# State-space units issued to TensorE in pairs, with the B and C transposes and chunk 8 moved

## The reference, cut to what matters

```
h = x * (1 + sc_m) + sh_m
u, q, k, v, g_out, a_low = jnp.split(h @ w_in[layer], IN_SPLITS, axis=-1)
y_s5  = _s5_group(u, ...)       # 32 groups of 16 channels, 64 complex states each
y_gla = _gla_group(q, k, v, g_out, a_low, ...)
y = jnp.concatenate([y_s5, y_gla], axis=-1) @ w_out[layer]

# in _s5_group
bu = jnp.einsum('gph,blgh->blgp', b_bar, u_c)        # B: channels to states
states = linear recurrence of bu over the sequence
y = jnp.einsum('ghp,blgp->blgh', c_mat, states).real # C: states to channels
y = jax.nn.gelu(y + d_skip * u);  return y * sigmoid(y @ w_glu + b_glu)
```

## Time and profile before

| what | value |
| --- | --- |
| median of 3 runs | 2751.89 us (2750.16 to 2752.95) |
| the profiled execution's own time | 2751.11 us |
| its span | 2749.3 us, 36615 instructions |
| PE busy | 2582.1 us, 94% of the span |
| DVE, ACT, POOL busy | 63%, 46%, 25% |
| mixer of layer 2, from the first projection matmul to the start of `y_sum(1)` | 888.12 to 997.15 us of the span |
| the same for layer 3 | 1349.90 to 1453.77 us |

### The profile page before, as it was taken

The page is one execution under the profiler, slowest core; times in us unless marked ns, Lnnn a source line. Parts: engine busy times, 40 slices in busy tenths (PEclk is TensorE's granted clock), DMA queues, the critical chain, the costliest instruction groups (busy, mean ns, idle before and its releaser), DMA issues.

```text
span 2749.3 us, 36615 instructions
## 1 busy us (share of the span) xinstructions
PE 2582.1 (94%) x14374; PEld 2086.1 (76%) x14374; DVE 1739.3 (63%) x1998; ACT 1257.4 (46%) x1300; POOL 675.9 (25%) x353
## 2 busy tenths in 40 slices
PE   7998999998999987999896699999999999999996
PEld 4775998874998754999774488888888878787884
DVE  1254665454866565665465577777777777777785
ACT  1123443223443112333112277677677777676763
POOL 0000000001920433920171122232223323222223
PEclk9998999998999998999997799999999999999997
DMA  9885764466774563875431299999999999999992
GB/s 339 274 282 192 253 215 143 153 217 204 242 228 153 174 209 123 265 226 184 124 113 35 70 364 341 357 329 367 329 369 329 359 337 348 350 348 340 344 360 106
DMA packets 434952, 693.80 MB, mean 252 GB/s; under 512 B 37690, under 2 KB 255894, under 8 KB 434838
## 3 DMA queue, kind: packets, MB, share of 16 engines
q1 hardware_dynamic: 407632, 677.17, 71.6%
q10 hardware_dynamic: 27206, 15.03, 2.0%
HBM read 691.10 MB, written 1.05 MB: 252 GB/s over the span
## 4 chain that ended last, share of the span: by engine, by line
PE 50%; issue 30%; POOL 11%; DVE 5%; ACT 2%; DMA 1%; SPq 0%; POOLq 0%; ACTq 0%; DVEq 0%
POOL ring_part L1260 10%; PE bank L656 9%; PE bank L788 9%; PE bank L790 8%; PE bank L789 8%; PE bank L560 3%; PE bank L772 3%; PE bank L670 3%; PE bank L898 1%; PE bank L543 1%; PE bank L719 1%; ACT hT L1368 1%; PE bank L918 1%; PE bank L751 1%; PE bank L633 1%
## 5 line engine op out<-in xcount | busy, mean ns | idle before, releaser
L1368 ACT ACTIVATE region_part<-ring 128x2048 fp32r<-128x2048 f32 x432 | 805.1, 1907 | 302.6 <-PE bank L790 197.7
L790 PE MATMUL bank<-ring_part,region_part 128*128 128x512 f32 x1648 | 649.1, 394 | 0.0
L2204 DVE TENSOR_TENSOR ring_part<-ring,region_part 128x2048 fp32r<-128x2048 f32 x270 | 640.4, 2404 | 2.8 <-ACT region_part L1368 2.8
L788 PE MATMUL bank<-region_part 128*128 128x512 f32 x1432 | 582.8, 407 | 6.2 <-DVE ring_part L2204 6.2
L789 PE MATMUL bank<-region_part 128*128 128x512 f32 x1296 | 512.1, 395 | 0.0
L1260 POOL TENSOR_TENSOR ring_part<-ring,region_part 128x2048 fp32r<-128x2048 f32 x54 | 268.7, 4983 | 554.5 <-ACT region_part L1368 554.5
L790 PEld LDWEIGHTS bank<-ring_part,region_part 128*128 128x128 f32 x1648 | 309.9, 188 | 71.4
L788 PE MATMUL bank<-xn_part,region_part 128*128 128x256 f32 x1152 | 327.8, 285 | 10.0 <-DVE hT_part L1924 9.1
L788 PEld LDWEIGHTS bank<-region_part 128*128 128x128 f32 x1432 | 269.7, 188 | 75.6 <-issue 14.6
L790 PE MATMUL bank<-hT_part,region_part 128*128 128x256 f32 x1152 | 326.0, 283 | 0.0
L789 PE MATMUL bank<-xn_part,ring_part 128*128 128x256 f32 x1152 | 325.7, 283 | 0.0
(11 more groups left out here) (295 smaller groups left out, 3432.1 us busy)
## 6 DMA issues: line engine op xcount, KB each, us to landing
ring<-in_moe_w_gate SPq DMA_DIRECT2D x126, 1024.0 KB, 5.1
ring<-in_moe_w_up SPq DMA_DIRECT2D x126, 1024.0 KB, 5.1
ring<-in_moe_w_down SPq DMA_DIRECT2D x126, 1024.0 KB, 5.0
ring<-in_w_ada SPq DMA_DIRECT2D x48, 1024.0 KB, 7.5
ring<-in_mod_w SPq DMA_DIRECT2D x48, 1024.0 KB, 5.3
ring<-in_w_in SPq DMA_DIRECT2D x44, 1024.0 KB, 5.7
ring<-in_w_up_act SPq DMA_DIRECT2D x22, 1024.0 KB, 5.4
ring<-in_w_up_lin SPq DMA_DIRECT2D x22, 1024.0 KB, 6.1
```

The costliest lines, as they stand in the source:

```text
L788: nc.tensor.matmul(o, split(a_hi), split(b_hi), start=start, stop=False, skip_group_check=True)
L790: return nc.tensor.matmul(o, split(a_hi), split(b_lo), start=False, stop=stop, skip_group_check=True)
L1368: return nc.scalar.activation(out_, in_, func, **kw).then_inc(*done(*event))
L2204: v.tensor_tensor(split(w), w, whole(hi), ALU.subtract).then_inc(*done("moe_lo", j, e))
```

## The change

`s5_in` and `s5_out` take two units at a time and issue their matmuls alternately. The loop over u becomes a loop over four pairs. Since both units of a pair are issued together, `s5_in` of a pair now waits for the banks of both units of the pair before (units u-2), and `s5_out` for both rotations. The transposes of B move between the two token halves of the norm's transposes, into banks 4 and 5, and those of C behind the second half, into banks 6 and 7. ACT copies the B matrices before it scales the norm's result. Chunk 0 comes first, and chunk 8 follows the first pair's `s5_in`; `alpha_low` follows chunk 1. The ada sums 8 to 11 follow chunk 7, ahead of the last `s5_out`. On DVE `gate_start` follows unit 2. The plan of chunks has the same chunks in PE's new order.

```diff
+S5_CHUNKS = [(8, 1), (2, 3), (4, 5), (6, 7)]
...
-            for n in (8, 0):
-                plan.append((("in", l, n), ("pe_tile", "in", l, n)))
-            for u in range(10):
...
+            plan.append((("in", l, 0), ("pe_tile", "in", l, 0)))
+            for p in range(len(S5_CHUNKS)):
+                for i, n in enumerate(S5_CHUNKS[p]):
+                    plan.append((("in", l, n), ("pe_tile", "in", l, n)))
+                    if l == 2:
+                        plan.append((("ada", 3, 2 * p + i), ("pe_used", "ada", 3, 2 * p + i)))
+            for q in range(8, 12):
...
             def mixer_two(l):
-                norm_tiles(l, "mix")
+
+                def b_turned():
+                    pe.wait_ge(*until("b_masked", l))
+                    for r in range(2):
+                        transposes(("BT", l, r), ("bst", l, r), [...], (4 + r,))
+
+                norm_tiles(l, "mix", b_turned)
+                for r in range(2):
+                    transposes(("CT", l, r), ("c_masked", l, r), [...], (6 + r,))
                 hT_ready(l, "mix")
...
-                in_features(l, 8, (4,))
...
                 in_features(l, 0, (4,))
...
-                def s5_in(u):
-                    qq, i = u // 4, u % 4
+                def s5_in(*pair):
+                    outs = [[bank(("bu", l, u, r), ("s5_g", l, u), (2 * (u % 2) + r,)) for r in range(2)] for u in pair]
                     for r in range(2):
-                        o = bank(("bu", l, u, r), ("s5_g", l, u), (2 * (u % 2) + r,))
                         for jj in range(2):
-                            q = 2 * qq + jj
-                            m = nc.tensor.matmul(o[:, jj * S:(jj + 1) * S], Bst[32 * i:32 * i + 32, r, q, :],
-                                                 uT[32 * i:32 * i + 32, q, :], start=True, stop=True)
-                        m.then_inc(*done("pe_tile", "bu", l, u, r))
+                            for u, o in zip(pair, outs):
+                                i, q = u % 4, 2 * (u // 4) + jj
+                                m = nc.tensor.matmul(o[r][:, jj * S:(jj + 1) * S], Bst[32 * i:32 * i + 32, r, q, :],
+                                                     uT[32 * i:32 * i + 32, q, :], start=True, stop=True)
+                                if jj:
+                                    m.then_inc(*done("pe_tile", "bu", l, u, r))
...
-                def s5_out(u):
+                def s5_out(*pair):
...
+                    for u in pair:
+                        pe.wait_ge(*until(*s5_rotated(l, u)))
...
                     for jj in range(2):
                         for r in range(2):
+                            for u in pair:
+                                i = u % 4
+                                m = nc.tensor.matmul(ys[qq][32 * i:32 * i + 32, jj * S:(jj + 1) * S],
+                                                     Cst[:, r, 2 * qq + jj, 32 * i:32 * i + 32], h5[:, u % 2, r, jj, :],
+                                                     start=r == 0, stop=r == 1, skip_group_check=True)
...
+                for p in range(4):
+                    if p == 2:
                         pe.wait_ge(*until("in_out", l, 1))
+                    s5_in(2 * p, 2 * p + 1)
+                    for i, n in enumerate(S5_CHUNKS[p]):
+                        if n in (8, 1, 2, 3):
+                            in_features(l, n, among)
+                        else:
+                            in_tokens(l, n, among)
+                        if l == 2:
+                            ada_sum(3, "mix", 2 * p + i, 0)
+                        if i == 0 and p:
+                            s5_out(2 * p - 2, 2 * p - 1)
+                    if p == 0:
                         alpha_low()
+                for q in range(8, 12):
                     if l == 2:
                         ada_sum(3, "mix", q, 0)
+                s5_out(6, 7)
...
-                    if u == 1:
+                    if u == 2:
                         gate_start()
```

More of the change, by code:

```diff
@@ L583, in norm_free, with norm_tiles @@
                 return ("hT", l, stage, b) if b % 2 == 0 else ("hTd", l, stage, b)
-            def norm_tiles(l, stage):
+            def norm_tiles(l, stage, between=None):
                 src = xn if l < 2 else x
@@ L603, in norm_tiles @@
                             m.then_inc(*done("norm_turned", l, stage))
+                    if t == 0 and between:
+                        between()
             def hT_ready(l, stage):
@@ L869, in mixer_two @@
             def mixer_two(l):
-                norm_tiles(l, "mix")
+                def b_turned():
+                    pe.wait_ge(*until("b_masked", l))
+                    for r in range(2):
+                        transposes(("BT", l, r), ("bst", l, r), [(q * P, Bnat[:, r, 4 * q:4 * q + 4, :].rearrange("p j c -> p (j c)")) for q in range(4)],
+                                   (4 + r,))
+                norm_tiles(l, "mix", b_turned)
+                for r in range(2):
+                    transposes(("CT", l, r), ("c_masked", l, r), [(q * P, Cnat[:, r, q, :]) for q in range(4)], (6 + r,))
                 hT_ready(l, "mix")
@@ L912, in s5_out @@
                         ys[qq] = psum[b]
-                    pe.wait_ge(*until(*s5_rotated(l, u)))
-                    if u == 0:
+                    for u in pair:
+                        pe.wait_ge(*until(*s5_rotated(l, u)))
+                    if pair[0] == 0:
                         pe.wait_ge(*until("cst", l))
@@ L917, in s5_out @@
                         for r in range(2):
[L918 to L921, removed]
+                            for u in pair:
[3 more added lines that the diff above has]
+                                                     start=r == 0, stop=r == 1, skip_group_check=True)
+                                if jj and r:
+                                    m.then_inc(*done("pe_tile", "s5o", l, u))
@@ L923, in mixer_two @@
                 pe.wait_ge(*until("bst", l, 1))
                 pe.wait_ge(*until("in_out", l, 0))
-                for u in range(10):
-                    if u == 4:
+                among = (4,) if l == 2 else (4, 5)
+                for p in range(4):
+                    if p == 2:
                         pe.wait_ge(*until("in_out", l, 1))
-                    if u < 8:
-                        s5_in(u)
-                    if u == 1:
-                        alpha_low()
[L932 to L938, removed]
-                        ada_sum(3, "mix", u, 0)
-                    if u >= 2:
-                        s5_out(u - 2)
@@ L1522, in mixer_two @@
             def mixer_two(l):
+                for r in range(2):
+                    p_ = tile("BT", l, r)
+                    run(Bst[:, r].rearrange("p c n -> p (c n)"), p_, ACT.Copy, "bst", l, r)
                 norm_out(l, "mix")
                 feats = {8: aT[0:16, :], 0: uT[:, 0:2, :], 1: uT[:, 2:4, :], 2: gqT, 3: gkT}
-                for n in (8, 0, 1, 2, 3):
+                for n in (0, 8, 1, 2, 3):
                     p_ = tile("in", l, n)
@@ L1528, in mixer_two @@
                     run(dst, p_[0:16, 0:S] if n == 8 else p_, ACT.Copy, "in_out", l, n, scale=0.125 if n == 2 else 1.0)
-                    if n == 8:
-                        for r in range(2):
-                            p_ = tile("BT", l, r)
-                            run(Bst[:, r].rearrange("p c n -> p (c n)"), p_, ACT.Copy, "bst", l, r)
                 act.wait_ge(*until("gla_abs", l))
```

6 lines of the change are left out of this document (2 added, 4 removed).

## The result

| what | before | changed |
| --- | --- | --- |
| median | 2752.42 us (2750.16 to 2753.96, 4 runs) | 2728.42 us (2727.02 to 2728.51, 4 runs) |
| span of the profiled execution | 2749.3 | 2726.5 |
| start of `y_sum(1)`, layer 2 | 997.15 | 983.02 |
| start of `y_sum(1)`, layer 3 | 1453.77 | 1431.08 |
| from there to the end of the span | 1295.5 | 1295.4 |

The change makes the kernel faster: ratio 0.9912, 95% interval 0.9901 to 0.9924, a gain of 24.0 us. The forecast was 26.9 and 2725.0. Five more runs of the changed kernel, made later beside two of the experiments, gave 2728.24.

A forecast was written before the change was run, and what follows sets the result against it. PE was taken to bound the kernel (busy 94% of the span), with DVE ending last in layer 3. Gains of 12.0 us in layer 2 and 14.9 in layer 3, 26.9 off 2751.89, gave 2725.0; range 2716.5 to 2736.

The forecast's parts named there:

- the forecast's bound with a second spell in each layer: Both layers: a further half-clock spell in each would leave a gain of 23.5 us, 2728.4.
- The price of a pair: `s5_in` and `s5_out`: a pair costs about what one unit does, 1.96 us in and 1.8 out.
- the column rival: `s5_out` pairs: columns do not overlap, each pair costs 1.8 us more; gain 14.3, 2737.6; chance 0.06.
- Front of the stage: Stage start: transposes hidden in waits, chunk 0 first at half clock; first pair at 898.7 and 1360.5.
- one spell less, 3.4 in both layers: Stage starts: if transposes in the waits shorten each half-clock start by one spell, another 3.4 us is gained.
- The new wait: Before pair (2, 3): PE waits for banks of units 0 and 1, 3.4 us in layer 2, about 5 in layer 3.
- One spell behind it: Behind the wait before pair (2, 3): one half-clock spell charged at 1.7 us in each layer.
- Rounds: After pair (2, 3): 18.0 us per round in layer 2, 16.0 in layer 3, plus 1.96 per pair in.
- DVE's end in layer 3: Layer 3's end: DVE ends last, 0.1 + 6.4 + 0.9 + 6.4 + 4.0 us, until 1436.9.
- The last `s5_out` of layer 3: Layer 3's end: follows DVE's end at 1436.9 and brings the stage to 1438.8, 14.9 us before 1453.77.
- Downstream moves as a block: GLU, GLA and feed-forward: same instructions, `y_sum(1)` to the end as long as before within 2 us per layer.
- Two of the signs: Profile after: layer 3 `y_sum(1)` near 1439, first `s5_in` near 1360.5; DVE's unit 7 scans end behind chunk 7 there.

The follow-up runs named there:

- e1: Changed kernel, but inside each pair all matmuls of the first unit are issued before the second's, in `s5_in` and `s5_out`; 2741.22 us, ratio 0.9969.
- e2: Changed kernel, but only the `s5_out` matmuls are issued unit by unit, `s5_in` still alternately; 2730.50 us, ratio 0.9933.
- second profile: Another profile of the unmodified changed kernel, run again later beside two experiments; median 2728.24 us, ratio 0.9915.
- e3: Changed kernel plus unread products filling PE's wait before pair (2, 3), 7 in layer 2 and 11 in layer 3; 2717.63 us, ratio 0.9887.
- e10: Changed kernel plus unread products in PE's wait before pair (2, 3), and `gate_sums` behind unit 4 instead of 5; 2718.56 us, ratio 0.9882.
- e11: As e10, plus eight more unread products ahead of layer 3's last `s5_out`; 2718.68 us, ratio 0.9881.

## Why the prediction was right

The time was 3.4 us above the forecast and inside the range; the mechanism, pairs that overlap plus transposes in waits, is the one forecast. That it came so near is in part luck: of the steps below, some were better than forecast by 4.8 us in all, others worse by about 9, and that the median of 2728.4 is also the forecast's bound with a second spell in each layer is a coincidence, since the front and layer 3's end had moved too. By its steps, each counted from the stage's last norm transposes:

- **The price of a pair**: right. 2.00 and 1.90, forecast 1.96 and 1.8. The *reason* was half right: the `alpha_low` and ada rows showed an overlap where the group changes, and I read from them that whole streams overlap. They do when they are issued alternately, but e1 and e2 were needed to tell; a kernel with grouped, unalternated units would have had 2.9 and 2.8, and I would have been wrong with the same evidence.
- **The Trainium skill's rule** (TensorE: Matmul & The Clock Gate, Part 3, "What overlaps and what doesn't"), that a weight load overlaps running matmuls only when the row group differs, is not borne out: on these shapes the pair out, all rows and another column group, took 1.90 alternated, 2.8 in sequence and 3.6 as two units before. The measurement decides, and the column rival falls.
- **Front of the stage**: forecast first pair 13.3 (layer 2) and 13.75 (layer 3) after the norm's transposes; it was 11.3 and 11.9. I charged chunk 0 with chunk 8's full loss to the clock, 2.8 and 2.3. The transposes in the wait keep PE busy, and the clock was up by 888 and 1338.9. The bound "one spell less, 3.4 in both layers" described this, and 3.9 came.
- **The new wait**: right, 3.44 and 5.31 against 3.4 and about 5.
- **One spell behind it** was the step that failed: the term was mis-sized. The loss was about twice the 1.7 us of one spell, 1.8 us in the pair and 2.1 in chunk 2 (1.3 for layer 2's chunk in the second profile), 3.9 in each layer. The granted clock was at 0.50 in one piece of some 8 us from the pair on. I had taken the price from the row where half clock began in a busy stretch (8.79 - 7.10). e3 shows that filling the wait removes it.
- **Rounds**: 19.86 us in layer 2 against 19.96, and 17.99 against 17.96 in layer 3. `gate_start` and the bunched ada sums' loads cost nothing.
- **DVE's end in layer 3** was the second miss. I had 6.4 + 0.9 + 6.4 + 4.0 and 0.1 for the stretch from the pair (6, 7) to the rotation's end, 17.8; it was 20.7. Unit 6 started 1.1 late behind a slowed `gate_sums`, and unit 7's rotation took 6.0 instead of 3.9, since POOL now rotates unit 6 at the same time. I had looked at DVE's and POOL's loads one by one and not at what they do to each other. In layer 2 the same slowdown is hidden by the ada sums.
- **The last `s5_out` of layer 3** took 3.54, not 1.9: another idle time, and half clock behind it.
- **Downstream moves as a block**: 1295.5 and 1295.4. True here, with the caution of e10 and e11. Between the two stages it was 349.6 and 350.8.
- **Two of the signs were written down wrong.** `y_sum(1)` "near 1439" and a first pair "near 1360.5" in layer 3 leave out the 12.0 us that layer 2 was to gain; with them it is about 1427 and 1348.5, and 1431.1 and 1345.8 came. And the sign has DVE's scans of unit 7 end behind chunk 7 in layer 3, while the forecast's own sum has only their rotation end behind it; so it was (scans 1421.2, chunk 7 1423.2, rotation 1427.3).

Sum for layer 2: 2.0 better at the front, 2.1 worse by the second spell, 0.9 better in the rounds and at the end: 12.6 for 12.0, two misses that nearly cancel. For layer 3: 1.9 better at the front, 2.1 for the second spell, 1.1 and 2.1 for DVE beside POOL, 1.6 for `s5_out`, in all some 5 worse: 9.8 for 14.9. By the second profile the two gains are 14.1 and 10.1.

## What to carry to other kernels

Small matmuls that use one row or column group can share the array with those of another: issue units on different groups alternately, matmul by matmul, since issuing them one behind the other brought only half here. Pairing units on one engine makes it wait for both units' buffers, so plan independent work for that wait in the same change; here the halves alone brought 5 and 6 us of the 24. And when an edit shifts one engine against another, check which operations now run at the same time on DVE and POOL, and what stands behind each of TensorE's new waits, because it may run at half clock.

## What the runs showed of the hardware that was not expected

- **DVE beside POOL.** With POOL working on SBUF, DVE's operations on SBUF alone took 1.38 to 1.78 us instead of 0.43 to 0.69, and the pair of scans 3.25 instead of 1.27. Operations with an operand in a PSUM bank did not change (0.68 to 0.70 from 1408.4 to 1411.6, while POOL ran). This agrees with the Trainium skill (SBUF — State Buffer, "Who interferes with whom"), which has the two engines share one SBUF port pair as an exclusive lock, taken by a DVE instruction with two SBUF inputs when POOL's reads SBUF; the scans too read two tensors in SBUF, `ones` and `region`. But the TENSOR_SCALAR reads one, and it slowed from 0.43 to 1.38 as well, which the rule of two inputs does not cover; the same section names `tensor_scalar` among the operations that can take the shared pair in a mode that uses both ports. That it takes 0.43 where the others take 0.69 fits, but no run here tests it.
- **Half clock after a short idle time, after hardly any, and not after each.** A wait of 3.4 us was followed by about 8 us at 0.50 with PE busy, and 4.2 us in front of a 1.9 us product by one of 3.5. In e1 a pair behind an idle time of only 0.82 us took 4.62 instead of 2.93, and in layer 3 2.93 us of idle time were followed by an `s5_out` of 4.44 instead of 2.81. In e2 the same place, with 3.08 us, stayed at a granted clock of 1.00. So the length of the idle time alone does not decide. Chunk 8 (16 columns of the array) and chunk 4 also slowed in e1, chunk 4 with PE busy all the time since the pair (2, 3); what set these off stays open.
- **The rest of a kernel is not fixed.** The same instructions behind the stage took 1291.1 to 1297.3 us in these kernels; the two profiles that were compared, e3's and e11's, differ in where the spells of half clock fell, and four executions of e3 alone spread over 4.7 us. For effects below some 5 us the stage's own rows are the better witness than the total.
